# Three root-mean-square norms with tokens on partitions, and weight splits moved ahead of a norm's pieces

## The chip, the cores and the metric

The kernel runs on one NeuronCore of a Trainium2 chip. Its time is device microseconds from launch to end, as the median of several runs. The engines run their own in-order queues and meet through semaphores: TensorE (PE; its weight loads are PEld), VectorE (DVE), ScalarE (ACT), GpSimd (POOL) and SyncE (SP, which issues most DMAs).

## What is computed

A trunk of two layers on an input of 1024 tokens by 1024 features, all float32. Layer 0 mixes tokens by a pooling mixer, layer 1 by an mLSTM (8 heads, here 16 head steps, since the tokens go in two halves). A squared-ReLU MLP follows each mixer. Every sub-layer stands between two norms:

```python
def rmsnorm(x, g):
    return x * lax.rsqrt(jnp.mean(x * x, axis=-1, keepdims=True) + RMS_EPS) * g

for i in range(DEPTH):                       # DEPTH = 2
    hn = rmsnorm(x, mix_pre_g[i])
    y = pool_mixer(hn, ...) if i % 2 == 0 else mlstm_mixer(hn, ...)
    x = x + rmsnorm(y, mix_post_g[i])
    hn = rmsnorm(x, ffn_pre_g[i])
    y = jnp.square(jax.nn.relu(hn @ mlp_w1[i])) @ mlp_w2[i]
    x = x + rmsnorm(y, ffn_post_g[i])
```

## The kernel before

**Layout.** Features lie on partitions: a half of the tokens (`T` = 512) of the activations is eight tiles `y[half][:, k, :]` of 128 features by 512 tokens. A norm therefore sums over partitions as well as over the eight tiles.

**Products.** A float32 product is made of three passes on rounded parts: weights are split into `w_hi` (a cast on ACT, `split_hi`) and `w_lo` (a subtraction on DVE, `split_lo`), activations into `x_hi` and `x_lo`, and PE does hi·hi, hi·lo and lo·hi of 512 columns each (`three_passes`, lines 787 to 789). A weight block must have both parts before PE may start it (`split_ready`). In the head steps, the call that splits `BLOCK["head", j, 2] + 1` makes the parts of the fourth block of head j.

**Norms.** There are 14. Norms 3 to 12 have their squares added on DVE (`acc`, line 1872) and summed over partitions by GpSimd (`partition_all_reduce`, line 1229). Norms 0, 1, 2 and 13 (`FOREGROUND`) are summed by PE: a plain float32 product of a square tile with the tile `ones` gives all 128 partitions the same sums for 512 tokens, in PSUM. Then ACT takes the root of 128x512 into `tot` (`root`, line 1280), DVE its reciprocal of 128x512 into `rstd` (line 1812), and DVE multiplies tile by tile (`normed`, line 1189).

**The opening.** Norm 0 is the norm behind the pooling mixer of half 0, norm 1 the one before the MLP of half 0. PE runs the list `SECOND_POOL`: W are window products of the other half (`window_tile`, line 821), T the sum of norm 0, S the eight sums of norm 1, G the eight groups of the mixer's product. Behind the last G, ACT takes its result out of PSUM (`pool_out`, line 1735), then makes `x_hi` of the first tile (line 1777), DVE its `x_lo` (line 2404), and PE starts the MLP (line 887).

**The head steps.** In step j PE does four weight blocks, each followed by a piece of work of head j-1: `turn`, `updates`, `numerators` (lines 1102 and 1106) and `turn_back` (line 1116). ACT and DVE do their parts in written order. Between them stand `tick(j, part)` calls, which do the pieces of two background norms that the table `LSTM_SLOTS` gives to this place: in steps 2 and 10 `tick(j, 1)` makes the last two additions to `acc`, upon which GpSimd's reduction starts, and in steps 4 and 12 two additions and two residual tiles. `normalize` writes `hnorm`, for which `turn_back` waits. `gate_head(j - 1)` writes `hid_hi` and `hid_lo`, which the output projection (`second_product`, line 851) reads in the step after; the next split is that projection's second block.

**The last head.** `last_head` runs the last head's pieces between pieces of the output projection. ACT does `by_tokens` (waits for `turn`, makes `kw` and `v_tok`) and then `decay_matrix` (four exponentials), for which DVE's `prob` and so PE's numerators wait.

**The end.** Norm 13 closes the kernel. PE sums five tiles into `bank[0]`, then multiplies the eight tiles of `x_last` with the identity into the eight PSUM banks, then the eight scaled tiles on top; so PE adds the residual. ACT copies each bank to `end_sq`, SP stores it.

Of the kernel before, what the change touches and what calls it, by code (L numbers as in the profile page):

```python
# [7 lines left out]
ALU = mybir.AluOpType  # L8
# [5 lines left out]
P = 128  # L14
D = 1024
# [216 lines left out]
def build(nc, x_in, x_tokens, weights, w_first, w_second, vecs_in, consts_in, bands_in, out):  # L232
# [9 lines left out]
    with ExitStack() as ctx:  # L242
# [122 lines left out]

        ones_row = relu_sq
# [44 lines left out]
        end_taken = sem("last_output_taken")  # L411
        x_first_landed = sem("first_old_x_landed")
# [110 lines left out]
        FOREGROUND = (0, 1, 2, 13)  # L523
        BACKGROUND = 3
# [6 lines left out]
        def last_bank(k):  # L531
            return eight[(k + 1) % KT]

# [109 lines left out]
        def _(sp):  # L643
# [105 lines left out]
            for k in range(KT):  # L749
                sp.wait_ge(end_taken, k + 1)  # L750
                sp.dma_start(out[1, k], end_sq[:, k, :]).then_inc(out_stored[1], 16)
# [4 lines left out]
        def _(pe):  # L756
# [14 lines left out]
            def sum_squares(n, tiles=range(KT), o=None, order=tuple(range(KT))):  # L771

                for k in tiles:
                    at = KT * FOREGROUND.index(n) + order.index(k)
                    pe.wait_ge(sq_ready, at + 1)
                    nc.tensor.matmul((o or core[3])[:, :], ones[:, :], (end_sq[:, k, :] if n == NORMS - 1 else squares[k]),
                                     start=(k == order[0]), stop=(k == order[-1])).then_inc(sq_summed, 1)
# [17 lines left out]
            def sum_added():  # L795

                pe.wait_ge(sq_added, KT - 1)
                nc.tensor.matmul(core[3][:, :], ones[:, :], squares[KT - 1], start=True, stop=True).then_inc(sq_summed, 1)
# [96 lines left out]
            def plain_second(layer):  # L895

                for k in range(PLAIN):
# [4 lines left out]
                    for d in ds:  # L902
                        if k == 0 and d < BANKS:
                            pe.wait_ge(plain_taken, layer * HALVES * PLAIN + plain_of_bank(layer, d, 0) + 1)
                        if k == 0 and d == KT - 1 and layer == 0:
# [246 lines left out]
            for step in SECOND_POOL:  # L1152
                if step == "T":
                    sum_added()
                elif step[0] == "W":
                    window_tile(1, int(step[1]))
                elif step[0] == "G":
# [12 lines left out]
            for at, k in enumerate(LAST_D[0:4]):  # L1170
                pe.wait_ge(sq_ready, KT * FOREGROUND.index(NORMS - 1) + at + 1)
                nc.tensor.matmul(bank[0][:, :], ones[:, :], end_sq[:, k, :],
                                 start=(at == 0), stop=False).then_inc(sq_summed, 1)
            pe.wait_ge(end_sums, 3)
            nc.tensor.matmul(bank[0][:, :], ones[:, :], end_sq[:, 3, :], start=False, stop=True).then_inc(sq_summed, 1)
# [1328 lines left out]
```

## Time and profile before

| | us |
|---|---|
| runs (median of 3) | 1971.12 (1970.82 to 1972.35) |
| the profiled execution | 1969.38 |
| its span, first to last instruction | 1967.6 |
| PE busy in it | 1932.8 |
| DVE busy | 1321.8 |
| ACT busy | 1064.2 |
| POOL busy | 91.0 |

The difference of 1.8 between the profiled execution and its span lies outside of the program's instructions. Times below are microseconds from the start of the span. A row of the timeline gives start, length, engine and line, operation, output<-inputs, the shape and the number of instructions merged, and in brackets how long the engine was idle before it and who ended that. `issue` means that the profile shows no releaser. The stages: opening to 66, MLP of layer 0 to about 745, head steps to about 1290, MLP of layer 1 to 1946, end.

### The profile page before, as it was taken

To read this page: it belongs to the slowest core of one execution; us is meant where nothing else is said; L and a number is where in the kernel's file an instruction comes from. 1 tells how busy PE (TensorE), PEld (TensorE's weight loads), DVE (VectorE), ACT (ScalarE), POOL (GpSimd) and SP (SyncE) were. 2 spreads that over 40 slices of the span, in tenths; PEclk is the share of its full clock that TensorE was granted. 3 is DMA by queue.
4 is the path that set the end of the run, shared out by engine and by line. 5 is a ranking of instruction groups with operands and counts; after the bars stand their busy time and mean duration, and the time that the engine had idled before them with its cause. 6 is when DMAs were issued, how large, how long until landed. Compare 5 with 4: busy or idle time off the path is not lost. (4 is left out here: it accounts for less than half of the span.)

```text
span 1967.6 us, 24435 instructions
## 1 busy us (share of the span) xinstructions
PE 1932.8 (98%) x8582; PEld 1546.2 (79%) x8582; DVE 1321.8 (67%) x2070; ACT 1064.2 (54%) x1803; POOL 91.0 (5%) x121
## 2 busy tenths in 40 slices
PE   9999999999999999999999999899999999999999
PEld 6678888888788788878878878777888888878786
DVE  5775656565678877776866857776656565577864
ACT  7645454554445446766756757544554545445433
POOL 0110000000000100110000100021000000000110
PEclk9999999999999999999999999999999999999999
DMA  5344234348633533343223442243524344853353
GB/s 213 103 157 177 103 136 161 134 177 297 229 94 103 197 111 100 118 150 97 97 77 104 135 135 96 66 150 119 191 91 163 132 165 172 315 186 97 112 196 115
DMA packets 80568, 283.94 MB, mean 144 GB/s; under 512 B 9504, under 2 KB 9632, under 8 KB 73536
## 3 DMA queue, kind: packets, MB, share of 16 engines
q1 hardware_dynamic: 64576, 237.86, 34.6%
q0 software_dynamic: 8320, 27.27, 4.3%
q10 hardware_dynamic: 7552, 17.26, 2.7%
q8 instruction: 69, 1.13, 0.2%
q14 instruction: 51, 0.42, 0.1%
HBM read 213.08 MB, written 69.27 MB: 144 GB/s over the span
## 5 line engine op out<-in xcount | busy, mean ns | idle before, releaser
L1807 DVE TENSOR_TENSOR w_lo<-raw,w_hi 128x1024 fp32r<-128x1024 f32 x148 | 185.8, 1256 | 188.5 <-ACT w_hi L1266 185.4
L1266 ACT CAST w_hi<-raw 128x1024 fp32r<-128x1024 f32 x148 | 154.3, 1042 | 195.7 <-PE core L1006 54.1
L787 PE MATMUL bank<-x_hi,w_hi 128*128 128x512 f32 x560 | 227.4, 406 | 7.0 <-issue 6.6
L1452 ACT CAST h_hi<-h_raw 128x512 fp32r<-128x512 f32 x178 | 110.3, 620 | 222.6 <-PE core L1006 137.5
L789 PE MATMUL bank<-x_hi,w_lo 128*128 128x512 f32 x560 | 221.7, 396 | 0.0
L788 PE MATMUL bank<-x_lo,w_hi 128*128 128x512 f32 x560 | 220.6, 394 | 0.0
L2062 DVE TENSOR_TENSOR h_lo<-h_raw,h_hi 128x512 fp32r<-128x512 f32 x178 | 122.9, 690 | 106.9 <-ACT h_hi L1452 106.5
L1004 PE MATMUL core<-h_hi,w_hi 128*128 128x512 f32 x448 | 177.9, 397 | 2.5 <-ACT w_hi L1468 2.5
L1006 PE MATMUL core<-h_hi,w_lo 128*128 128x512 f32 x448 | 176.8, 395 | 0.0
L1005 PE MATMUL core<-h_lo,w_hi 128*128 128x512 f32 x448 | 176.5, 394 | 0.0
L1956 DVE TENSOR_TENSOR w_lo<-sums,w_hi 128x512 fp32r<-128x512 f32 x96 | 66.3, 691 | 99.7 <-ACT w_hi L1294 97.1
L787 PEld LDWEIGHTS bank<-x_hi,w_hi 128*128 128x128 f32 x560 | 105.3, 188 | 32.5 <-issue 10.1
L1004 PE MATMUL bank<-h_hi,w_hi 128*128 128x512 f32 x328 | 129.9, 396 | 0.0
L1006 PE MATMUL bank<-h_hi,w_lo 128*128 128x512 f32 x328 | 129.4, 395 | 0.0
L1005 PE MATMUL bank<-h_lo,w_hi 128*128 128x512 f32 x328 | 129.4, 394 | 0.0
L789 PEld LDWEIGHTS bank<-x_hi,w_lo 128*128 128x128 f32 x560 | 105.1, 188 | 25.7
L788 PEld LDWEIGHTS bank<-x_lo,w_hi 128*128 128x128 f32 x560 | 105.3, 188 | 23.8 <-issue 0.7
L2100 DVE TENSOR_TENSOR w_lo<-w,w_hi 128x512 fp32r<-128x512 f32 x160 | 114.0, 713 | 12.7 <-ACT w_hi L1468 8.7
L887 PE MATMUL bank<-x_hi,w_hi 128*128 128x512 f32 x256 | 104.9, 410 | 3.2 <-DVE x_lo L2404 2.2
L1468 ACT CAST w_hi<-w 128x512 fp32r<-128x512 f32 x160 | 98.4, 615 | 14.8 <-DMA w<-second_pairs 5.7
L1004 PEld LDWEIGHTS core<-h_hi,w_hi 128*128 128x128 f32 x448 | 84.1, 188 | 23.9 <-issue 4.1
L1229 POOL PARTITION_ALL_REDUCE tot<-acc x10 | 34.5, 3447 | 1477.8 <-DVEq L1876 1477.8
(333 smaller groups left out, 4444.2 us busy)
## 6 DMA issues: line engine op xcount, KB each, us to landing
raw<-weights SPq DMA_DIRECT2D x148, 512.0 KB, 3.3
h_pair_dram<-y SPq DMA_DIRECT2D x24, 1792.0 KB, 6.6
h_raw<-h_pair_dram SPq DMA_DIRECT2D x168, 256.0 KB, 2.8
w<-second_pairs SPq DMA_DIRECT2D x32, 768.0 KB, 4.5
x_scratch<-y POOLq DMA_DIRECT2D x48, 256.0 KB, 2.6
raw_odd<-first_pairs SPq DMA_DIRECT2D x12, 1024.0 KB, 7.1
raw<-first_pairs SPq DMA_DIRECT2D x12, 1024.0 KB, 7.1
xold<-x_scratch POOLq DMA_DIRECT2D x40, 256.0 KB, 3.8
```

The source lines that it names most:

```text
L787: nc.tensor.matmul(o, a, hi(t), start=(k == 0), stop=False)
L788: nc.tensor.matmul(o, a, lo(t), start=False, stop=False)
L789: last = nc.tensor.matmul(o, b, hi(t), start=False, stop=(k == n - 1))
L887: nc.tensor.matmul(o, a, XH(half, k), start=(k == 0), stop=False)
L1004: nc.tensor.matmul(o[:, :], a, hh, start=(fresh and first), stop=False, skip_group_check=True)
L1005: nc.tensor.matmul(o[:, :], a, hl, start=False, stop=False, skip_group_check=True)
L1006: ins = nc.tensor.matmul(o[:, :], b, hh, start=False, stop=(final and last), skip_group_check=True)
L1266: nc.scalar.copy(w_hi[:, ROW[u] * T:(ROW[u] + 2) * T], raw[:, (n % RAW) * BLK:(n % RAW + 1) * BLK]).then_inc(hi_ready, 1)
L1452: nc.scalar.copy(h_slot(n)[0], h_raw[:, at % H_RAW, :]).then_inc(h_hi_ready, 1)
L1807: dve.tensor_tensor(w_lo[:, s], raw[:, (n % RAW) * BLK:(n % RAW + 1) * BLK], w_hi[:, s].bitcast(F32), ALU.subtract).then_inc(lo_ready, 1)
L2062: dve.tensor_tensor(lo, h_raw[:, at % H_RAW, :], hi.bitcast(F32), ALU.subtract).then_inc(h_lo_ready, 1)
L2100: dve.tensor_tensor(w_lo[:, s], second_weight(n), w_hi[:, s].bitcast(F32), ALU.subtract).then_inc(lo_ready, 1)
```

## The change

It has three parts.

1. Norms 0, 1 and 13 (`BY_TOKEN`) put tokens on partitions. `token_sums` makes the square tile the stationary operand, in four pieces of 128 tokens, and moves `ones` of 128 columns through; the result is 128 equal columns for each group of 128 tokens. ACT takes the root of one column of each (128x4), DVE the reciprocal of 128x4 and multiplies the identity with it into four diagonal 128x128 tiles in `step_t`; `spread_roots` then multiplies `ones` with the four diagonals, which gives the 128x512 factor in PSUM (`core[3]`, `bank[0]` for norm 13), and `normed` reads it there. `SECOND_POOL` gets R0 and R1 for the two `spread_roots`. The sums of norms 1 and 2 move from `core[3]` to `core[2]`.
2. In the head steps `split_hi` and `split_lo` of the fourth block go ahead of `tick(j, 1)`; for j = 4, 8, 12 `gate_head(j - 1)` goes ahead of `tick(j, 2)`; for the last head `decay_matrix` goes ahead of `by_tokens`.
3. At the end tiles 2, 5 and 7 (`END_ADDED`) get their residual by DVE instead of by PE and ACT. PE does the other five.

```diff
-SECOND_POOL = "W0 T W1 W2 W3 W4 W5 W6 W7 S0 S1 G0 G1 S2 S3 G2 S4 G3 S5 S6 S7 G4 G5 G6 G7".split()
+SECOND_POOL = "W0 T W1 W2 R0 W3 W4 W5 W6 W7 S0 S1 G0 G1 S2 S3 G2 S4 G3 S5 S6 S7 G4 R1 G5 G6 G7".split()
+END_ADDED = (2, 5, 7)
...
+            def token_sums(n, tile, first, last):
+                for c in range(CPH):
+                    ins = nc.tensor.matmul(norm_sums(n)[:, c * P:(c + 1) * P], tile[:, c * P:(c + 1) * P], ones[:, :],
+                                           start=(first and c == 0), stop=(last and c == CPH - 1),
+                                           skip_group_check=True)
+                ins.then_inc(sq_summed, 1)
+
+            def spread_roots(n):
+                for c in range(CPH):
+                    pe.wait_ge(diag_ready, CPH * BY_TOKEN.index(n) + c + 1)
+                    ins = nc.tensor.matmul(norm_roots(n)[:, c * P:(c + 1) * P], ones[:, :], step_t[:, c * P:(c + 1) * P],
+                                           start=True, stop=True)
+                ins.then_inc(rstd_ready, 1)
...
-            for k in range(KT):
-                if k == KT - 1:
-                    pe.wait_ge(std_ready, NORMS)
-                nc.tensor.matmul(last_bank(k)[:, :], ident, x_last[:, k, :], start=True, stop=False)
-            for k in range(KT):
-                pe.wait_ge(end_scaled, k + 1)
-                nc.tensor.matmul(last_bank(k)[:, :], ident, y[1][:, k, :], start=False, stop=True).then_inc(end_done, 1)
+            old(tiles[0])
+            old(tiles[1])
+            spread_roots(NORMS - 1)
+            for at in range(2, len(tiles)):
+                old(tiles[at])
+                add(at - 2)
+            add(len(tiles) - 2)
+            add(len(tiles) - 1)
...
+                    if n in BY_TOKEN:
+                        nc.scalar.activation(token_std.rearrange("p (c o) -> p c o", o=1),
+                                             src[:, :].rearrange("p (c t) -> p c t", c=CPH)[:, :, 0:1], ACT.Sqrt, bias=eps[:, :],
+                                             scale=1.0 / D).then_inc(std_ready, 1)
+                        return
...
-                        by_tokens(j - 1)
                         decay_matrix(j - 1)
+                        by_tokens(j - 1)
...
-                dve.reciprocal(rstd[:, :], tot[:, :]).then_inc(rstd_ready, 1)
+                steps.finish(dve.reciprocal(token_rstd, token_std))
+                for c in range(CPH):
+                    dve.tensor_scalar(step_t[:, c * P:(c + 1) * P], ident, token_rstd[:, c:c + 1], None,
+                                      ALU.mult).then_inc(diag_ready, 1)
...
                     states(j - 1)
+                    split_lo(BLOCK["head", j, 2] + 1)
                     tick(j, 1)
-                    split_lo(BLOCK["head", j, 2] + 1)
...
+                    if j % FT == 0:
+                        gate_head(j - 1)
                     tick(j, 2)
-                    gate_head(j - 1)
+                    if j % FT:
+                        gate_head(j - 1)
...
+                steps.finish(scaled)
+                dve.wait_ge(x_last_landed, 16)
+                dve.tensor_tensor(end_sq[:, k, :], x_last[:, k, :], y[1][:, k, :], ALU.add).then_inc(end_added, 1)
```

DVE in head step 2, from the chunk states (`mid`) to the next head's convolution (`win`). Before:

```order
L2236 SCALAR_TENSOR_TENSOR mid<-mid,inter_b,core1 128x129
L1872 TENSOR_TENSOR acc<-acc,sq 128x512 x2
L1807 TENSOR_TENSOR w_lo<-raw,w_hi 128x1024
L2201 COPY craw<-taps 128x16
L2202 COPY taps<-craw 128x16
L2207 SCALAR_TENSOR_TENSOR win<-craw,vecs,win 128x512 x3
```

Now, with the line numbers of the changed kernel:

```order
L2293 SCALAR_TENSOR_TENSOR mid<-mid,inter_b,core1 128x129
L1858 TENSOR_TENSOR w_lo<-raw,w_hi 128x1024
L1929 TENSOR_TENSOR acc<-acc,sq 128x512 x2
L2258 COPY craw<-taps 128x16
L2259 COPY taps<-craw 128x16
L2264 SCALAR_TENSOR_TENSOR win<-craw,vecs,win 128x512 x3
```

The two additions to `acc`, which release GpSimd's reduction, now stand directly ahead of the convolution instead of ahead of the split. Steps 4, 6, 7 and their twins of the second half change in the same way, with other pieces in the place of the additions.

DVE in head step 4, behind the blocks of head 4. Before:

```order
L2289 TENSOR_TENSOR qs<-qT,inter_b 128x512
L1872 TENSOR_TENSOR acc<-acc,sq 128x512
L1189 SCALAR_TENSOR_TENSOR step_t<-y1,vecs,rstd 128x512
L1884 TENSOR_TENSOR y1<-xold,step_t 128x512
L2274 SCALAR_TENSOR_TENSOR relu_sq<-oT,core0 128x512
L2277 TENSOR_SCALAR hid_hi<-relu_sq,half_norm 128x512
L2278 SCALAR_TENSOR_TENSOR hid_lo<-relu_sq,half_norm,hid_hi 128x512
L1807 TENSOR_TENSOR w_lo<-raw,w_hi 128x1024 x5
```

Now:

```order
L2346 TENSOR_TENSOR qs<-qT,inter_b 128x512
L2331 SCALAR_TENSOR_TENSOR relu_sq<-oT,core0 128x512
L2334 TENSOR_SCALAR hid_hi<-relu_sq,half_norm 128x512
L2335 SCALAR_TENSOR_TENSOR hid_lo<-relu_sq,half_norm,hid_hi 128x512
L1929 TENSOR_TENSOR acc<-acc,sq 128x512
L1236 SCALAR_TENSOR_TENSOR step_t<-y1,vecs,rstd 128x512
L1941 TENSOR_TENSOR y1<-xold,step_t 128x512
L1858 TENSOR_TENSOR w_lo<-raw,w_hi 128x1024 x5
```

The three instructions of `gate_head` went ahead of the norm's three; the splits behind them stay last.

PE at the end, behind the last product of the MLP. Before (ten of the sixteen rows with the identity; the other six are alike but for the bank):

```order
L1172 MATMUL bank0<-end_sq,ones 128x512 x4
L1175 MATMUL bank0<-end_sq,ones 128x512
L1181 MATMUL bank1<-x_last,consts 128x512
L1181 MATMUL bank2<-x_last,consts 128x512
L1181 MATMUL bank3<-x_last,consts 128x512
L1181 MATMUL core0<-x_last,consts 128x512
L1181 MATMUL core1<-x_last,consts 128x512
L1181 MATMUL core2<-x_last,consts 128x512
L1181 MATMUL core3<-x_last,consts 128x512
L1181 MATMUL bank0<-x_last,consts 128x512
L1184 MATMUL bank1<-y1,consts 128x512
L1184 MATMUL bank2<-y1,consts 128x512
```

Now:

```order
L789 MATMUL bank0<-ones,end_sq 128x128 x20
L1217 MATMUL bank1<-x_last,consts 128x512
L1217 MATMUL bank2<-x_last,consts 128x512
L798 MATMUL bank0<-step_t,ones 128x128 x4
L1217 MATMUL core0<-x_last,consts 128x512
L1221 MATMUL bank1<-y1,consts 128x512
L1217 MATMUL core1<-x_last,consts 128x512
L1221 MATMUL bank2<-y1,consts 128x512
L1217 MATMUL core3<-x_last,consts 128x512
L1221 MATMUL core0<-y1,consts 128x512
L1221 MATMUL core1<-y1,consts 128x512
L1221 MATMUL core3<-y1,consts 128x512
```

Sixteen products with the identity became ten, and the four that spread the roots stand behind the second of them.

## Rows read from the trace of the kernel before

**Rows 1.** The page's first part: busy us, share of the span, number of instructions.
```profile
PE 1932.8 (98%) x8582; PEld 1546.2 (79%) x8582; DVE 1321.8 (67%) x2070; ACT 1064.2 (54%) x1803; POOL 91.0 (5%) x121
```
**Rows 2.** Waits of PE over the span: us in total, times, longest.
```profile
PE bank L787 <- issue: 6.6, 7, 1.8
```
**Rows 3.** Timeline of PE in the opening: start, length, what.
```profile
37.69 0.38 PE L821 MATMUL core<-sq,y 128*128 128x128 f32 x2
37.91 0.29 PE L815 MATMUL core<-kw,qT 128*128 128x16 f32 x2
```
**Rows 4.** Timeline of DVE in the opening.
```profile
37.65 3.35 DVE L1812 RECIPROCAL rstd<-tot 128x512 f32<-128x512 f32 x1 [1.28 <-ACT tot L1280]
```
**Rows 5.** Timeline of PE in the opening, two waits.
```profile
48.74 0.48 PE L787 MATMUL bank<-x_hi,w_hi 128*128 128x512 f32 x1 [0.40 <-DVE x_lo L1845]
...
57.69 1.12 PE L776 MATMUL core<-craw,ones 128*128 128x512 f32 x2 [0.21 <-ACT craw L1712]
```
**Rows 6.** Timeline of all engines where the MLP starts.
```profile
65.13 0.60 ACT L1777 CAST x_hi<-y 128x512 fp32r<-128x512 f32 x1
...
66.60 0.47 PE L887 MATMUL bank<-x_hi,w_hi 128*128 128x512 f32 x1 [2.19 <-DVE x_lo L2404]
```
**Rows 7.** Line 1695, a root of 128x4: shortest, median, longest in ns.
```profile
L1695 ACT ACTIVATE small<-small,eps x16: 297/297/298, 779.5 to 1270.0; 128x4 f32<-128x4 f32 x16
```
**Rows 8.** Line 2264, a product of 128x128 with a per-partition factor.
```profile
L2264 DVE TENSOR_SCALAR hnorm<-core,small x64: 339/343/353, 780.3 to 1271.6; 128x128 f32<-128x128 f32 x64
```
**Rows 9.** Timeline of all engines at the end.
```profile
1950.60 2.74 PE L1181 MATMUL bank<-x_last,consts 128*128 128x512 f32 x6
...
1950.80 0.69 ACT L1280 ACTIVATE tot<-bank,eps 128x512 f32<-128x512 f32 x1 [2.94 <-PE bank L1175]
...
1954.91 5.39 DVE L1189 SCALAR_TENSOR_TENSOR y<-y,vecs,rstd 128x512 f32<-128x512 f32 x8
...
1964.53 0.59 ACT L1792 COPY end_sq<-bank 128x512 f32<-128x512 f32 x1 [0.27 <-PE bank L1184]
```
**Rows 10.** DMA issues: line, count, KB each, median us to landing.
```profile
out_tiles<-end_sq SPq DMA_DIRECT2D x8, 256.0 KB, 2.0
```
**Rows 11.** Timeline of ACT in the last head.
```profile
1258.62 1.15 ACT L1675 ACTIVATE kw<-core,cols 128x128 f32<-128x128 f32 x4 [3.35 <-PE core L1080]
...
1261.56 1.28 ACT L1661 ACTIVATE mx_b<-mx_b,cols 128x128 f32<-128x128 f32 x4
```
**Rows 12.** Timeline of DVE in the last head.
```profile
1264.95 0.34 DVE L2236 SCALAR_TENSOR_TENSOR mid<-state,inter_b,core 128x129 f32<-128x129 f32 x1
```
**Rows 13.** A stretch of the last head: length, PE busy, granted clock, DMA share, GB/s.
```profile
1263.60:1267.00 3.40, 3.31 (x13) 0.50 0.27 84
```
**Rows 14.** Timeline of DVE in head step 2.
```profile
799.82 1.49 DVE L1872 TENSOR_TENSOR acc<-acc,sq 128x512 f32<-128x512 f32 x2
802.40 2.38 DVE L1807 TENSOR_TENSOR w_lo<-raw,w_hi 128x1024 fp32r<-128x1024 f32 x1 [1.09 <-ACT w_hi L1266]
```
**Rows 15.** Timeline of PE in head step 2.
```profile
804.88 0.47 PE L787 MATMUL bank<-x_hi,w_hi 128*128 128x512 f32 x1 [0.78 <-issue]
...
810.67 0.66 PE L1116 MATMUL core<-consts,hnorm 128*128 128x128 f32 x4
```
**Rows 16.** Timeline of POOL in head step 2.
```profile
801.46 3.23 POOL L1229 PARTITION_ALL_REDUCE tot<-acc  x1 [111.74 <-DVEq L1876]
```
**Rows 17.** Timeline of DVE at the start of an earlier reduction.
```profile
632.49 2.73 DVE L2100 TENSOR_TENSOR w_lo<-w,w_hi 128x512 fp32r<-128x512 f32 x1 [0.21 <-DVE acc L1872]
```
**Rows 18.** Timeline of ACT in head step 4.
```profile
855.94 0.63 ACT L1545 ACTIVATE qT<-win 128x512 f32<-128x512 f32 x1
```
**Rows 19.** Timeline of DVE in head step 4.
```profile
861.14 1.22 DVE L1807 TENSOR_TENSOR w_lo<-raw,w_hi 128x1024 fp32r<-128x1024 f32 x1
...
874.77 1.22 DVE L1807 TENSOR_TENSOR w_lo<-raw,w_hi 128x1024 fp32r<-128x1024 f32 x1
```
**Rows 20.** Timeline of PE in head step 4.
```profile
874.91 0.50 PE L851 MATMUL bank<-hid_hi,w_hi 128*128 128x512 f32 x1 [1.04 <-DVE hid_lo L2278]
```

More of the change, by code:

```diff
@@ L523, in build @@
         FOREGROUND = (0, 1, 2, 13)
+        BY_TOKEN = (0, 1, 13)
         BACKGROUND = 3
@@ L749, in _ @@
             for k in range(KT):
-                sp.wait_ge(end_taken, k + 1)
+                if k in END_ADDED:
+                    sp.wait_ge(end_added, END_ADDED.index(k) + 1)
+                else:
+                    sp.wait_ge(end_taken, k + 1 - sum(a < k for a in END_ADDED))
                 sp.dma_start(out[1, k], end_sq[:, k, :]).then_inc(out_stored[1], 16)
@@ L769, in keep_clock, with sum_squares @@
                     nc.tensor.matmul(o[:, :], ones[:, :], ones_row[:, :], start=True, stop=True)
-            def sum_squares(n, tiles=range(KT), o=None, order=tuple(range(KT))):
-                for k in tiles:
[L774 to L777, printed above, removed]
+            def token_sums(n, tile, first, last):
[10 more added lines that the diff above has]
+                ins.then_inc(rstd_ready, 1)
+            def sum_squares(n, tiles):
+                for k in tiles:
+                    pe.wait_ge(sq_ready, KT * FOREGROUND.index(n) + k + 1)
+                    if n == 1:
+                        if k == 0:
+                            pe.wait_ge(pooled_ready, KT + 3)
+                        token_sums(n, squares[k], k == 0, k == KT - 1)
+                    else:
+                        nc.tensor.matmul(norm_sums(n)[:, :], ones[:, :], squares[k],
+                                         start=(k == 0), stop=(k == KT - 1)).then_inc(sq_summed, 1)
             def three_passes(g, row, cols_of, hi, lo, tiles, before=None, after=None):
@@ L904, in plain_second @@
                             pe.wait_ge(plain_taken, layer * HALVES * PLAIN + plain_of_bank(layer, d, 0) + 1)
-                        if k == 0 and d == KT - 1 and layer == 0:
+                        if k == 0 and eight[d] is norm_sums(2) and layer == 0:
                             pe.wait_ge(std_ready, 3)
@@ L1156, in _ @@
                     window_tile(1, int(step[1]))
+                elif step[0] == "R":
+                    spread_roots(int(step[1]))
                 elif step[0] == "G":
@@ L1213, in add_residual @@
             for k in range(KT):
-                scaled = steps.begin(normed(eng, step_t[:, :], y[half][:, k, :], post + k))
+                scaled = steps.begin(normed(eng, step_t[:, :], y[half][:, k, :], post + k, norm_roots(0)))
                 low(k)
@@ L1789, in _ @@
             root(norms.pop(0))
-            for k in range(KT):
-                act.wait_ge(end_done, k + 1)
+            for at, k in enumerate(k for k in range(KT) if k not in END_ADDED):
+                act.wait_ge(end_done, at + 1)
                 nc.scalar.copy(end_sq[:, k, :], last_bank(k)[:, :]).then_inc(end_taken, 1)
```

40 lines of the change are left out of this document (29 added, 11 removed).

## The prediction

> **What bounds the kernel now.** I read the page's busy times first: TensorE works 1932.8 of a span of 1967.6, 98%, and VectorE only 67% [rows 1]. So work taken from VectorE or ScalarE is worth nothing in itself; only TensorE's own work, the places where it waits, and the two ends of the kernel count. The waits of TensorE come next. The line that the splits of weights could be blamed for shows 6.6 in seven waits, the longest 1.8 [rows 2]; one of them is the 0.78 in head step 2 [rows 15]. That is the most that splitting earlier can give back. The rest was read place by place, in the timelines of the stretches that the change touches. The profiled execution took 1969.38, 1.74 under the median of 1971.12. I make the sum against the profiled execution and add it to the median.
>
> **Norms 0 and 1 in the opening.** A plain float32 product takes TensorE 0.22 for 128 columns [rows 3], so a square tile costs 4 x 0.22 = 0.88. That is what 512 columns cost in one piece: three products in 2.74 with their modelled end, 0.86 each without it [rows 9]. The sums are therefore free to within 0.02 each. The reciprocal of 3.35 [rows 4] and a root of 128x512, 0.69 [rows 9], become a root of 0.30 [rows 7], a short reciprocal (about 0.2, bounded by 0.3, the ScalarE root of the same shape) and four diagonals of 0.34 or less [rows 8], then four products of 0.22: 0.30 + 0.2 + 1.4 + 0.9 = 2.8 instead of 4.0, so the factor comes about 1 earlier. But TensorE pays 4 x 0.22 = 0.88 for each `spread_roots`, 1.8 for both. What can absorb it are waits: 0.40 and 0.21 [rows 5], with the pipeline's own refill 0.8 to 0.9 for both. The big one, 2.19 ahead of the MLP [rows 6], does not shrink: it runs from TensorE's last group over ScalarE's copy, `x_hi` (65.13 to 65.73) and VectorE's `x_lo`, and R1 stands ahead of that last group, so that the whole chain moves with TensorE. Net 1.8 − 0.85 = **+1.0** (0 if the earlier factor also feeds the groups sooner, 1.8 if the two waits stay).
>
> **Head step 2, and its twin, step 10.** Before, VectorE adds to `acc` from 799.82 to 801.31, GpSimd's reduction starts at 801.46, and `w_lo` starts at 802.40, when ScalarE has written `w_hi`; it takes 2.38 [rows 14, 16]. Its normal length is 1.22 [rows 19]. So it was held by 1.16. If it was held in its first part, then until 803.56, 2.1 behind the start of the reduction of 3.23. An earlier reduction's start shows the same: 2.73 for a subtraction of 512 columns [rows 17], about half of 1.22 if alone, again held by about 2.1. Now `w_lo` comes first. It cannot start before 802.40, since `w_hi` is no earlier, but nothing holds it: it ends at 803.6 and TensorE's wait of 0.78 goes. The two additions follow until about 805.1, and the reduction starts at 805.2. That is exactly where the convolution stands: two copies and three passes over `win` with both tensors in SBUF, 0.3 behind their old place (old start 802.40 + 2.38 = 804.78). If they are held as `w_lo` was, they wait until 805.2 + 2.1 = 807.3, against 805.0: +2.35 with what is late already. Everything down to `hnorm` stands behind them in VectorE's order, and `turn_back` of TensorE (810.67 before [rows 15]) waits for `hnorm`. It then starts at 813.0, though TensorE is there almost 1 earlier. Behind `turn_back` TensorE has no other wait to give this back. So +2.35 each, **+4.7** for both. The low end, if nothing in SBUF is held, is +0.35 each, +0.7.
>
> By the Trainium skill, page "SBUF — State Buffer", section "Who interferes with whom", a VectorE instruction with two SBUF inputs and a GpSimd instruction that reads SBUF exclude each other, and the second to start blocks until the other is done. The row of `w_lo` agrees that there is an exclusion, but by the full reduction it should have run until 804.69 + 1.22 = 805.9, and it ended at 804.78 [rows 14, 16]. Going by that rule, each of the two places would cost 1.1 more.
>
> **Head steps 4 and 12.** ScalarE's `w_hi` comes behind `qT` (855.94 to 856.5 [rows 18]) and takes 1.0, so `w_lo` starts at 857.5 instead of 861.14 [rows 19], and a wait of TensorE of 1.8 (the longest of [rows 2]) is gone. But the pieces of the norm (two additions, two residual tiles, 4.6 in all with their gaps, being what stood between) now stand between `w_lo` and the convolution, which therefore starts at about 863.3 where it started at 861.14 + 1.15 = 862.3: the chain to `hnorm` is +1.0, while TensorE comes 1.8 earlier, and waits there instead, some 3.0. `gate_head` ahead of the next pieces then takes away a wait of 1.04 for `hid_lo` [rows 20], but puts a norm's three passes between it and the next splits: the `w_lo` that stood at 874.77 [rows 19] and ended at 876.0, just in time, ends at about 877.5. I take **+1.3** for step 4 and **+0.8** for step 12, where the old wait was 0.35 longer; −1.8 each if the convolution had slack after all, +2.4 each at worst (1.0 and 1.5 one after the other, nothing absorbed). In the other head steps the swap of split and pieces lies under TensorE's blocks of 5.8 with room on both sides: 0, and 0.3 each if the cover is gone.
>
> **The last head.** ScalarE idles for 3.35 ahead of `kw` and makes the four exponentials only from 1261.56 to 1262.84 [rows 11]. Both they and the load of their table fit into that idle time. So VectorE's `prob`, TensorE's numerators, and the split that follows come earlier; the chunk state at 1264.95 [rows 12] moves to about 1262.4, as `w_hi` and `w_lo` then end there: −2.5. TensorE's 3.31 of work here ran at a granted clock of 0.50, which is 1.2 of 2.4 GHz, behind its wait for the numerators [rows 13]; at the full clock it is up to 1.65 less, of which I take 0.7. **−3.2** (−2.2 to −3.5).
>
> **The end.** TensorE is the bound there: 16 products with the identity from 1950.60, about 0.86 each, and ScalarE's last copy ends at 1964.53 + 0.59 = 1965.12 [rows 9]. Now ten products, 8.6, and 0.9 of spreading: TensorE could be done at 1960.1. The factor is ready at 1950.8 + 0.3 + 0.2 + 1.4 + 0.9 = 1953.6, against 1954.9. VectorE then scales eight tiles in 5.4 [rows 9] and adds three residuals, 0.7 to 0.8 each: 1953.6 + 7.7 = 1961.3. VectorE takes TensorE's place as the bound, the last copy or addition ends at about 1961.6, −3.5. The last stores, 256 KB and 2.0 each [rows 10], go out closer together, which I price at +0.5 (0 to 1), and the sums at +0.1: **−2.8** (−3.4 to −2.3).
>
> **The clock.** The granted clock fell to 0.50 behind one wait of 2.14 in the last head (the numerators') and for 3.4 [rows 13], that is up to 1.7 lost. It did not fall behind the 2.19 of the opening in the profile I have [rows 6]. The change makes four waits of about 3 at `turn_back`. I take one fall, **+1.7** (0 to 6.8).
>
> **Sum**: 1.0 + 4.7 + 1.3 + 0.8 − 3.2 − 2.8 = +1.8; with the clock +3.5. 1971.1 + 3.5 = **1974.6**.
>
> **Rivals.** (a) The convolution is held, but the clock stays: 1971.1 + 1.8 = 1972.9. The opening's wait of 2.19 without a fall speaks for it. Chance 0.13. (b) The convolution is not held: 4.0 less and less of the wait that lowers the clock, so 1968.9. For it speaks that three of five instructions have a factor per partition beside their tensors and the copies are only 16 columns wide; against it, that all the data are in SBUF as those of the held `w_lo`. Chance 0.18. (c) The waits of the heads vanish and nothing is late behind them: 1.0 − 3.2 − 2.8 = −5.0, 1966.1, and as low as 1955.5 if all the waits of [rows 2] and their followers go too. It needs slack between the convolution and `hnorm`, which the rows of step 2 do not show. Chance 0.09. (d) The slower side: all four long waits halve the clock, each for 3.4, 4 x 1.7 = 6.8 on +1.8: 1979.7. It decides from the point where a wait at `turn_back` passes 2.2 or so, the longest that a row shows without a fall; mine are about 3. Chance 0.10. (e) The hold lasts for the whole reduction instead of 2.1: 1.1 more at two places, 1974.6 + 2.2 = 1976.8. `w_lo` speaks against it, since it ended early. Chance 0.05. It is what the page named above would give, and the trace does not agree.
>
> The forecast itself has 0.45: held at both places, one or two falls of the clock, 1973 to 1977.
>
> **How the numbers follow.** A measurement of this kernel can tell about 0.2%, 3.9, from no change: faster is below 1967.2, slower above 1975.1. Faster: (c), and a quarter of (b): 0.14. Slower: (d), (e), and somewhat under half of the forecast, whose centre lies half a microsecond below the line: 0.35. The same: 0.51. The range reaches from (b) and the upper part of (c), 1966.5, to 1978.0, which leaves out (d) and the lower half of (c).
>
> **What would show it.** In the changed kernel's trace: `w_lo` of step 2 takes 1.2 and TensorE's wait behind it is gone; the reduction starts right behind it at about 805 and one of the convolution's instructions lasts 2 too long; TensorE waits about 3 for `hnorm` in steps 2, 4, 10 and 12; the granted clock is 0.50 behind one of them; in the last head the numerators stand directly behind the updates and the chunk state is 2.5 earlier, relative to the head's start; the last copy ends about 3.5 earlier relative to the last sum, and VectorE, not TensorE, ends last. The MLP's first wait is still 2.2, 1.0 later. The forecast is wrong if the convolution runs at its normal length beside the reduction (then 1969), or if the waits at `turn_back` stay under 1.

## The result, and the profile after

The changed kernel takes 1977.58 us (median of 8 runs, 1975.88 to 1980.02) against 1970.97 for the kernel before (8 runs, 1969.66 to 1972.35): 1.0037 times as long, 95% interval 1.0027 to 1.0047. It is slower by 5.3 to 9.3 us, 6.6 in the medians. The forecast was 1974.6, that is +3.5, and the likeliest single verdict was "the same". The profiled execution took 1979.08, 1.5 above the median, with a span of 1977.3. All differences below are between the profiled executions unless a median is named.

Three words are used throughout. The *lag* at a place is how much later the same product of TensorE starts in one trace than in the other. A *fall* is a stretch in which the granted clock is 0.50, that is 1.2 GHz in place of 2.4. An instruction is *held* when it lasts longer than the same instruction does elsewhere in the trace.

The page's first part, as in [rows 1]: TensorE's busy time is 6.7 longer, while the change takes work away from it at the end.

```profile
PE 1939.5 (98%) x8678; PEld 1560.3 (79%) x8678; DVE 1317.2 (67%) x2085; ACT 1060.7 (54%) x1800; POOL 91.2 (5%) x121
```

TensorE's waits (us in total, times, longest). The waits for a split, 6.6 in [rows 2], are down to 1.8, as was meant; a new line stands first in their place.

```profile
PE core L1151 <- DVE hnorm L2321: 13.8, 5, 3.5
PE bank L945 <- ACT h_plain L1407: 2.8, 2, 2.4
...
PE bank L822 <- issue: 1.8, 2, 1.1
```

**Head step 2.** The timeline of VectorE and GpSimd. Compare it with [rows 14, 16]: `w_lo` takes 1.22 instead of 2.38, the additions stand behind it, the reduction starts at 808.02, and the second copy of the convolution, 16 columns wide, takes 2.10 where its twin, which was under way when the reduction started, took 0.17.

```profile
805.24 1.22 DVE L1858 TENSOR_TENSOR w_lo<-raw,w_hi 128x1024 fp32r<-128x1024 f32 x1 [2.68 <-ACT w_hi L1313]
806.39 1.48 DVE L1929 TENSOR_TENSOR acc<-acc,sq 128x512 f32<-128x512 f32 x2
808.01 0.17 DVE L2258 COPY craw<-taps 128x16 f32<-128x16 f32 x1
...
808.02 3.27 POOL L1276 PARTITION_ALL_REDUCE tot<-acc  x1 [116.43 <-DVEq L1933]
...
808.22 2.10 DVE L2259 COPY taps<-craw 128x16 f32<-128x16 f32 x1
```

TensorE's rows at `turn_back` in steps 2, 4, 10 and 12. In [rows 15] the same row had no wait.

```profile
815.90 1.11 PE L1151 MATMUL core<-consts,hnorm 128*128 128x128 f32 x4 [3.48 <-DVE hnorm L2321]
875.54 0.66 PE L1151 MATMUL core<-consts,hnorm 128*128 128x128 f32 x4 [3.05 <-DVE hnorm L2321]
1100.23 1.11 PE L1151 MATMUL core<-consts,hnorm 128*128 128x128 f32 x4 [3.22 <-DVE hnorm L2321]
1160.95 1.12 PE L1151 MATMUL core<-consts,hnorm 128*128 128x128 f32 x4 [3.05 <-DVE hnorm L2321]
```

The four products take 1.11 or 1.12 in three of the four places, 0.66 in the other. That is the clock: at 875.54 it had not fallen yet. Stretches behind these waits, and behind two that the kernel before has as well (columns: from and to, length, busy us of PE, PEld, DVE, ACT and POOL with their instructions, then the granted clock, DMA share and GB/s):

```profile
815.50:819.00 3.50, 3.04 (x9) 2.28 (x10) 3.35 (x7) 3.47 (x5) 0.00 (x0) 0.53 0.28 62
876.40:880.60 4.20, 3.88 (x10) 3.08 (x11) 4.01 (x8) 0.98 (x3) 0.00 (x0) 0.59 0.39 125
1100.20:1106.20 6.00, 5.90 (x16) 4.52 (x17) 5.28 (x7) 4.70 (x6) 0.00 (x0) 0.53 0.27 90
1161.00:1167.50 6.50, 6.44 (x17) 4.94 (x18) 6.03 (x9) 3.26 (x6) 0.00 (x0) 0.52 0.25 81
68.00:72.00 4.00, 4.00 (x9) 2.50 (x10) 3.92 (x6) 3.54 (x8) 0.00 (x0) 0.57 0.02 4
1353.60:1358.60 5.00, 4.62 (x13) 3.65 (x14) 2.46 (x4) 2.63 (x4) 1.87 (x1) 0.66 0.38 129
```

All four long waits are followed by the 1.2 GHz level, and so are the MLP's first wait in the opening (2.19, at full clock in the kernel before, [rows 6]) and the wait of 2.37 for `h_plain` near 1354.

**The ledger.** I compared the starts of the same product in both traces (the 7632 products of 512 columns with `w_hi` or `w_lo` stand in the same order) and took the lag at a few places. The third column is what the lag grows by while the products behind a wait run at the half clock, the second is all the rest.

| stretch | lag grows by, clock apart | by the half clock | forecast |
|---|---|---|---|
| opening, to the MLP's first product | +1.4 | +1.5 | +1.0 |
| layer 0, a wait that absorbs | −0.5 | | |
| head step 2 | +2.8 (−0.73, then +3.54) | +0.9 | +2.35 |
| head step 4 | −0.1 (−2.00, +3.11, −1.19) | +1.5 | +1.3 |
| head step 10 | +2.5 (−0.83, +3.28) | +2.0 | +2.35 |
| head step 12 | −0.3 (−2.03, +3.12, −1.40) | +2.2 | +0.8 |
| last head (with the fall that went, [rows 13]) | −3.4 | | −3.2 |
| MLP of layer 1 | +0.3 | +1.6 | |
| end | −2.6 | | −2.8 |
| sum | +0.1 | +9.7 | +1.8, and +1.7 for the clock |

The sum is, but for rounding, the 9.7 between the spans. Without the falls behind its own waits the change is worth nothing; with them it costs 9.7 in this execution and 6.6 in the medians (this execution is 1.5 above its median, the one profiled before 1.6 below its own).

The +0.1 still holds one gain by the clock. In the last head the kernel before ran its numerators at 0.50 [rows 13]; from the first of them to the next block they took 3.60 (1263.67 to 1267.27), and here 2.53 at full clock, a new wait of 0.56 among them. So about 1.6 of the −3.4 is a fall that went. An estimate from these numbers: with no fall in either kernel the change would cost about 1.7.

**The last head.** The same stretch as [rows 11, 12], from VectorE and ScalarE: the exponentials now stand ahead of `kw`, and the first chunk state, which came 6.3 behind `kw`'s start, comes 3.7 behind it.

```profile
1270.47 1.28 ACT L1712 ACTIVATE mx_b<-mx_b,cols 128x128 f32<-128x128 f32 x4
1272.46 0.69 DVE L2276 SCALAR_TENSOR_TENSOR prob<-core,mx_b 128x512 f32<-128x512 f32 x1 [0.83 <-PE core L1115]
1272.51 1.15 ACT L1726 ACTIVATE kw<-core,cols 128x128 f32<-128x128 f32 x4 [0.77 <-issue]
1276.25 0.35 DVE L2293 SCALAR_TENSOR_TENSOR mid<-state,inter_b,core 128x129 f32<-128x129 f32 x1
```

**The end**, as in [rows 9]. TensorE's first product with the identity stands at 1963.09 here, at 1950.60 before. From there to the end of ScalarE's last copy it was 14.5, and it is 10.8. ScalarE's copy of TensorE's last tile ends last (1973.86); VectorE is through 0.4 earlier, but it sets the pace, since TensorE waits for each scaled tile.

```profile
1963.29 0.26 ACT L1323 ACTIVATE ssq<-bank,eps 128x4 f32<-128x4 f32 x1 [3.11 <-PE bank L789]
1963.59 0.18 DVE L1866 RECIPROCAL rs<-ssq 128x4 f32<-128x4 f32 x1 [1.95 <-ACT ssq L1323]
1963.80 0.87 DVE L1868 TENSOR_SCALAR step_t<-consts,rs 128x128 f32<-128x128 f32 x4
1964.81 1.05 PE L798 MATMUL bank<-step_t,ones 128*128 128x128 f32 x8
1965.90 2.06 DVE L1236 SCALAR_TENSOR_TENSOR y<-y,vecs,bank 128x512 f32<-128x512 f32 x3 [1.23 <-PE bank L798]
...
1973.27 0.59 ACT L1843 COPY end_sq<-core 128x512 f32<-128x512 f32 x1 [0.52 <-PE core L1221]
```

### The profile page after: what moved, and what is told of

It reads as the page before. It is cut to its first block and busy times, and to the rows that moved or that the text cites. A ratio compares the mean times of both kernels' runs of the same rounds, so it can differ in the third digit from the quotient of the medians.

```text
span 1977.3 us, 24651 instructions
## 1 busy us (share of the span) xinstructions
PE 1939.5 (98%) x8678; PEld 1560.3 (79%) x8678; DVE 1317.2 (67%) x2085; ACT 1060.7 (54%) x1800; POOL 91.2 (5%) x121
## 5 line engine op out<-in xcount | busy, mean ns | idle before, releaser
L1520 ACT CAST w_hi<-w 128x512 fp32r<-128x512 f32 x160 | 98.6, 616 | 13.8 <-DVE w L2137 4.6
```

## The experiments

Three theories stood: (A) the head steps' new order costs all of the loss, by a held convolution and a late chain, and each long wait brings a fall of the clock with it; (B) the norms with tokens on partitions cost it; (C) the falls are chance and only the waits count. The kernel before ran at 1969.90, 1970.65 and 1970.59 in the three groups of four.

### Which part costs it

**e1_old_order** is the changed kernel with the old order in the head steps, on VectorE (shown) and on ScalarE.

```diff
-                    split_lo(BLOCK["head", j, 2] + 1)
                     tick(j, 1)
+                    split_lo(BLOCK["head", j, 2] + 1)
...
-                    if j % FT == 0:
-                        gate_head(j - 1)
                     tick(j, 2)
-                    if j % FT:
-                        gate_head(j - 1)
+                    gate_head(j - 1)
```

> The changed kernel with the head steps back in their old order (split behind the pieces, gate_head behind them in every step); the last head, the three norms and the end stay changed. My ledger of the changed kernel's trace puts +11.6 us on head steps 2, 4, 10 and 12 (extra waits of TensorE for hnorm of 3.0 to 3.5 and the half clock behind each). If that is right, all of it goes: 1971.0 + 2.5 (opening) - 3.4 (last head) - 2.6 (end) = about 1967.5, between 1966 and 1969.5, and no wait over 2.0 in the head steps. Rival (the norms with tokens on partitions cost it, the order is innocent): 1975 or more.

Measured: 1966.31 (10 runs), 0.9981 of the kernel before (0.9971 to 0.9990). That is 3.6 faster than before, where the whole change is 6.6 slower. So (A) holds as to the place, and (B) is out: the order in the head steps costs about 10. Its waits of TensorE have the split first again, and none for `hnorm` above 1:

```profile
PE bank L822 <- issue: 7.1, 7, 1.9
```

One part of the expectation missed: there is a fall in its head steps, behind the wait for a split in step 12 (1.91); the kernel before has 1.78 there, without a fall.

**e3_opening_old_too** also takes norms 0 and 1 back.

```diff
-        BY_TOKEN = (0, 1, 13)
+        BY_TOKEN = (13,)
...
```

> As the first kernel, and norms 0 and 1 of the opening also as before; only the last head's swap and norm 13 with the end stay changed. Theory: 1971.0 - 3.4 - 2.6 = 1965. The difference to the first kernel is the opening's price: theory 1.0 to 1.4 at full clock (two times four products of 0.22 less what waits absorb), up to 2.5 with a fall of the clock behind the MLP's first wait. Rival: the opening costs nothing in itself and the 2.5 in the profile was the clock alone; then both kernels agree within 0.5.

Measured: 1963.71 (8 runs), 0.9970 (0.9959 to 0.9981), 6.2 faster than the kernel before. The two parts that are left, the last head and the end, are worth what the ledger says: the last head −3.37 in its trace too. Against e1 the opening costs 2.6 in the medians. The traces, at full clock in both at this place, put it at 1.2; with intervals of about 2 either way on each median I go by the traces. So the opening is not free, and the second case of the expectation is out, as far as one pair of traces can tell.

### The held convolution

**e2_adds_behind** makes the two additions of steps 2 and 10 behind `normalize`, so that the reduction doesn't meet the convolution.

```diff
-                    tick(j, 1)
+                    if j not in (2, 10):
+                        tick(j, 1)
                     conv(j, 1)
                     denominators(j - 1)
                     normalize(j - 1)
+                    if j in (2, 10):
+                        tick(j, 1)
```

> The changed kernel, but in steps 2 and 10 VectorE makes the two additions that release GpSimd's reduction behind normalize, not ahead of the convolution. If the convolution is held by the reduction (theory), the copy of taps takes 0.2 instead of 2.1, the two waits of about 3.4 at turn_back go, with the half clock behind them: 1977.6 - 2 x (2.4 + 0.35 + about 1.5) = about 1969, with up to 1.5 more if the earlier split is then worth its 0.75. Rival 1 (the waits cost only themselves, the clock fell by chance): 1972.5. Rival 2 (the additions themselves made the chain late, not the hold): the same gain as the theory in time, but then a held instruction would stand elsewhere in these steps at equal cost.

Measured: 1973.18 (10 runs), 1.0017 (1.0008 to 1.0026). That is 3.3 slower than the kernel before beside it, where the changed kernel was 6.6 slower: a gain of 3.3 (4.4 between the plain medians of the two), not the 8.6 expected. The copy of `taps` takes 0.17 again and the wait at `turn_back` is gone, so the hold was the cause of that wait. But a new wait stands behind `turn_back`. VectorE, GpSimd and TensorE in step 2:

```profile
813.55 1.23 DVE L1858 TENSOR_TENSOR w_lo<-raw,w_hi 128x1024 fp32r<-128x1024 f32 x1
813.55 4.31 POOL L1276 PARTITION_ALL_REDUCE tot<-acc  x1 [120.98 <-DVEq L1933]
814.69 2.73 DVE L2342 TENSOR_TENSOR mx_b<-consts,mx_b 128x512 f32<-128x512 f32 x1
...
814.87 0.48 PE L822 MATMUL bank<-x_hi,w_hi 128*128 128x512 f32 x1 [2.16 <-ACT w_hi L1313]
```

The `w_lo` of the block behind `turn_back`, which used to follow `hnorm` at once, came 1.6 late, and this wait (2.16, in step 10 2.03) halved the clock as well, in both steps. The reduction was held too: it started together with `w_lo` and took 4.31 instead of 3.27. I had moved the additions from in front of one thing that TensorE waits for to in front of the next one.

**e5_adds_behind_split** puts them one place further, behind that split.

```diff
                     split_lo(BLOCK["head", j, 3] + 1)
+                    if j in (2, 10):
+                        tick(j, 1)
```

> The changed kernel, but in steps 2 and 10 VectorE makes the two additions behind the split that follows normalize (in the last experiment of this kind they stood ahead of it, and TensorE got a new wait of 2.2 to 2.3 for that split). Theory (the hold of the convolution is all that was wrong there): no wait over 1 in steps 2 and 10, the chain 0.75 earlier than in the kernel before, since the split stands ahead: 1977.6 - 5.2 - 5.2 (the waits and one fall of the clock each) - up to 0.8 more = about 1967 to 1970, against the kernel before at 1969.9 on this chip. Rival (the reduction, now beside mx_b and qs, holds something that TensorE needs): a new wait of 2 in the step after, and 1972 or more.

Measured: 1968.87 (10 runs), 0.9991 (0.9981 to 1.0000). That is 1.8 faster than the kernel before beside it, so 8.4 better than the changed kernel (8.7 between the plain medians): the theory's case. The reduction now holds `qs`, which costs TensorE only 0.7 at the next head's first split:

```profile
811.50 1.22 DVE L1858 TENSOR_TENSOR w_lo<-raw,w_hi 128x1024 fp32r<-128x1024 f32 x1
812.63 1.49 DVE L1929 TENSOR_TENSOR acc<-acc,sq 128x512 f32<-128x512 f32 x2
814.26 0.69 DVE L2342 TENSOR_TENSOR mx_b<-consts,mx_b 128x512 f32<-128x512 f32 x1
814.87 2.73 DVE L2346 TENSOR_TENSOR qs<-qT,inter_b 128x512 f32<-128x512 f32 x1
```

The hold is 1.9 or 2.0 beyond the instruction's own length in these places (copy 2.10 for 0.17, `mx_b` in e2 and `qs` in e5 2.73 for 0.69). Steps 2 and 10 together are worth 8.4: the 2.8 and 2.5 of the ledger, the rest the clock (2.9 there).

### Steps 4 and 12

**e6_steps_4_12_new** and **e7_gate_first** start from the kernel of e3. The first has the whole new order in steps 4 and 12 only, the second only `gate_head` ahead of the next pieces:

```diff
+                    if j % FT == 0:
+                        gate_head(j - 1)
                     tick(j, 2)
-                    gate_head(j - 1)
+                    if j % FT:
+                        gate_head(j - 1)
```

> The kernel of e3_opening_old_too (1963.7) with the new order (split ahead of the pieces, gate_head ahead of the next ones) in steps 4 and 12 alone. Theory: two waits of 3.0 at turn_back in place of 1.9 ahead of it, hid_lo's wait of 1.0 to 1.4 gone: about +0.1 each at full clock, and a fall of the clock of 1.7 each: 1963.7 + 3.6 = 1967.3. Rival (the falls are not tied to these waits): 1964.

> The kernel of e3_opening_old_too with only gate_head ahead of the pieces in steps 4, 8 and 12. Forecast of the prediction: hid_lo's wait goes (1.0 and 1.4) but the split behind comes 1.5 late: about -0 to +0.5 per step. What the changed kernel's trace suggests: the wait goes and nothing comes in its place, -1.1 each in steps 4 and 12: 1961.5.

Measured: e6 1967.49 (10 runs), 0.9985 (0.9976 to 0.9995), as forecast, with both falls in the trace. e7 1964.32 (6 runs), 0.9970 (0.9959 to 0.9982), not the 1961.5. The split in step 4 of e7, and TensorE, which waits for it:

```profile
875.03 0.69 DVE L1939 TENSOR_TENSOR y<-xold,step_t 128x512 f32<-128x512 f32 x1
876.52 1.23 DVE L1856 TENSOR_TENSOR w_lo<-raw,w_hi 128x1024 fp32r<-128x1024 f32 x1 [0.79 <-ACT w_hi L1308]
...
877.85 0.47 PE L817 MATMUL bank<-hid_hi,w_hi 128*128 128x512 f32 x1 [1.40 <-issue]
```

The wait of [rows 20] is gone (−1.2), and 1.5 is lost behind it for the next split; in step 12 it is −1.6 and +1.6. This is just what the prediction said of it ("ends at about 877.5", here 876.52 + 1.23 = 877.75). In the changed kernel it can't be seen, because TensorE, at half clock, comes late enough. Its trace had misled me: a fall of the clock had covered a wait. That it was the fall and nothing else is argued from the two traces; no profile has the new order in step 4 at full clock.

**e8_combined** is e7 with e5's order in steps 2 and 10, **e9_best** the same without `gate_head`'s move.

> The kernel of e7 with the split ahead and the additions behind the next split in steps 2 and 10. If e5's theory and e7's second case both hold: -0.75 twice and -1.1 twice on 1963.7: 1960.0. If only one of them: 1961.5 to 1962.2.

> The kernel of e8_combined with gate_head behind the pieces again. e7 against e3 showed hid_lo's wait of 1.2 gone and a new one of 1.36 for the split behind it, 1.5 in all at two places, so the swap costs 0.3 each: 1964.0 - 0.6 = 1963.4 by that. Rival (the swap is worth something once steps 2 and 10 are clean): 1964.5 or more. The two can hardly be told apart by medians; the ledger of steps 4 and 12 in the trace tells them apart.

Measured: e8 1964.03 (6 runs), 0.9967 (0.9956 to 0.9979); e9 1963.98 (5 runs), 0.9966 (0.9952 to 0.9980). Neither differs from e3's 0.9970. In e9's trace steps 2 and 10 gain 1.0 and 1.1 up to `turn_back` and lose 0.6 and 0.7 at the next head's first block, whose split now waits for the additions and the held `qs`. So the earlier split is worth 0.4 a step at best in any order tried here, too little for these medians to show.

### The end

**e10_end_by_pe** is e3 with TensorE adding seven of the eight tiles.

```diff
-END_ADDED = (2, 5, 7)
+END_ADDED = (7,)
```

> The kernel of e3_opening_old_too, but only tile 7 gets its residual by VectorE; TensorE does seven (tile 7's bank holds the factor, so it can't be TensorE's). Theory (TensorE bounds the end, and each tile it gives up saves two products of 0.86 less what VectorE adds): 14 products and 0.9 instead of 10 and 0.9: the end 3.4 longer by TensorE, of which the changed end loses back its stores' crowding (about 0.9): 1963.7 + 2.5 = 1966.2. Rival (the gain came from the factor being early, not from sharing): 1963.7 to 1964.2.

Measured: 1967.68 (10 runs), 0.9985 (0.9975 to 0.9994), a ratio 0.0015 above e3's, or 2.9 us. The rival, that the early factor makes the gain, is out: from the first product with the identity (1948.65) to the end of the last copy it is 14.0, against 10.8 in e3.

```profile
1948.65 1.88 PE L1212 MATMUL bank<-x_last,consts 128*128 128x512 f32 x4
...
1962.02 0.58 ACT L1838 COPY end_sq<-core 128x512 f32<-128x512 f32 x1 [0.27 <-PE core L1216]
```

So the sharing of the additions makes most of the end's gain; against the 14.5 of the kernel before, what is left for the small root, the spreading and the one shared tile together is 0.5.

### What a wait does to the clock

Three kernels measured the disputed price by itself. They are the kernel before with products of `hnorm` repeated (the same values again), which makes TensorE wait at `turn_back` in nine head steps that had no wait there: graded numbers in e4, six each in e11, twelve each in e12.

```diff
+                for _ in range(EXTRA.get(j + 1, 0)):
+                    steps.finish(dve.tensor_scalar(hnorm[:, 0:LC], core[2][:, 0:HEAD_DIM], small[:, 7, 0:1], None,
+                                                   ALU.mult))
```

> The kernel before, with repeated products of hnorm's first 128 columns (0.3 to 0.4 each, the same values again) in nine head steps that wait for nothing now: 3 of them ahead of step 3's hnorm, 5 in step 5, 7 in 6, 9 in 7, 11 in 9, 4 in 11, 6 in 13, 8 in 14, 10 in 15. TensorE then waits at turn_back, from below 1 to about 4. Theory: behind each wait above about 2.2 the granted clock falls to 0.50 and costs 1.2 to 2.2 more; below 1.5 it never falls. So the total is the sum of the waits plus about 1.7 for each of the four or five long ones: some 7 over the waits. Rival: the falls have nothing to do with a wait's length; then some short waits show one and some long ones none, and the time is the sum of the waits within 2.

> The kernel before with six repeated products ahead of hnorm in each of nine head steps (3, 5, 6, 7, 9, 11, 13, 14, 15). By the graded run a wait of TensorE is 0.385 for each less 1.2: about 1.1 each. Theory: hardly any fall of the clock behind these (0 to 2 of 9): 1970.3 + 8 or 9 x 1.1 = 1980 (1979 to 1983). Rival (any wait can bring a fall): 1985 or more.

> The same with twelve in each of the nine steps: waits of about 3.4. Theory: every one is followed by a fall that costs 1.7: 1970.3 + 9 x (3.4 + 1.7) = 2016, and nine stretches at 0.50. Rival (falls are a matter of chance at any length): about half of them, 2008; or none beyond those that were there: 2001.

Measured: e4 1999.89, e11 1996.35, e12 2024.92 (4 runs each), that is +30.0, +25.8 and +54.3 on the kernel before. The waits for `hnorm` in e11 and e12 (in total, times, longest):

```profile
PE core L1118 <- DVE hnorm L2269: 10.8, 9, 1.5
```
```profile
PE core L1118 <- DVE hnorm L2269: 31.6, 9, 3.8
```

e11 missed its forecast of 1980 by 16. Some 5 of that I had overlooked in the trace of e4: behind a wait at `turn_back` TensorE waits again, 0.52, for the next block's split, which stands behind `hnorm` on VectorE. Some 7 are falls: four that the kernel before does not show, one of them behind waits of only 1.1 and 0.8 in a row. The other 3 or 4 lie between the profiled execution (1992.8) and the median; more falls would make them, which no profile shows. In e4, too, the expectation was too sharp: a wait of 1.5 had a fall ("below 1.5" was my limit) and one of 2.7 had none. In e12 every one of the nine waits is followed by a fall, five of them by a second directly behind the first; its time is 9 above the 2016 expected, by these second falls and by the 0.52 behind each wait, which that sum also left out. Stretches behind the first two waits of e12 (3.75 and 3.4) and behind the same waits of e11 (1.43 and 1.13):

```profile
841.50:848.00 6.50, 5.85 (x16) 4.47 (x17) 6.06 (x11) 0.63 (x1) 1.07 (x2) 0.53 0.35 121
928.70:933.70 5.00, 4.12 (x14) 3.19 (x15) 4.82 (x9) 1.84 (x3) 0.00 (x0) 0.66 0.32 105
```
```profile
839.50:846.00 6.50, 5.49 (x25) 4.37 (x26) 6.06 (x11) 1.99 (x3) 1.07 (x2) 1.00 0.37 121
923.10:929.10 6.00, 5.03 (x23) 3.99 (x24) 5.82 (x10) 4.23 (x5) 0.00 (x0) 1.00 0.27 90
```

I then read the granted clock in the 7 us behind every wait of TensorE of 1.3 or more in all 14 profiles, from 20 us on, and counted behind how many it was 0.50. A wait is here the figure in brackets of TensorE's row:

| wait of TensorE | waits | with a fall behind it |
|---|---|---|
| 1.3 to 1.99 | 29 | 4 |
| 2.0 to 2.4 | 37 | 21 |
| 2.6 to 2.9 | 3 | 2 |
| 3.0 and more | 18 | 18 |

A fall costs up to 1.7, and a second one directly behind it up to 1.7 more; it is less where a fall begins within the wait, as at 1099 in the changed kernel. Of the four below 2.0 three had another wait of 0.5 right behind them (so had some without a fall); the fourth is the 1.91 of e1. Between 2.0 and 2.4 the same wait goes both ways: the MLP's first wait, 2.19 in every profile, was followed by a fall in 6 of 14, the wait of 2.37 for `h_plain` in 8 of 14. What decides there stays open. These stretches are from behind the first of them, in e7 and in e8:

```profile
66.20:71.20 5.00, 4.50 (x11) 2.80 (x11) 4.86 (x8) 4.52 (x9) 0.00 (x0) 0.66 0.00 0
```
```profile
66.20:71.20 5.00, 4.49 (x16) 2.90 (x16) 4.86 (x8) 4.53 (x9) 0.00 (x0) 1.00 0.00 0
```

So (C) is right for waits of 2.0 to 2.4 and wrong for the change's own, which are 3.0 and more.

## Where the prediction failed, and what in it held

**The step that failed is the clock's.** It said: "The change makes four waits of about 3 at `turn_back`. I take one fall, +1.7 (0 to 6.8)." The waits came as forecast (3.48, 3.05, 3.22, 3.05), and each was followed by a fall, two of them by a double one: 6.6 in the ledger for these four, where the sum had 1.7. The rival (d), all four, was the right case in its mechanism; its 1979.7 is 2.1 above the median, because steps 4 and 12 cost less than the sum has. It got 0.10 because I compared waits of 3 with one of 2.19 that happened to have no fall in the one profile I had. Two waits of 2.1 to 2.3, one with a fall and one without, say that the matter is open at that length; for 3 they say that it can't be less likely. The likeliest case should have been (d). The other 3.1 of half clock in the profile are the falls behind the MLP's first wait and the wait for `h_plain`. Each comes in about half of the profiles, so I take them as chance, and in the median only in part.

**The held convolution**: right in place, instruction and size. The reduction started right behind the additions (808.02), and a copy of the convolution was held until 810.32. From `w_lo` to the last passes of the convolution VectorE fell 2.4 further behind in both steps (`w_lo` 802.40 and 805.24, `win` 804.99 and 810.23), forecast 2.35. TensorE's own lag grew by 2.8 in step 2, since it entered this step 0.4 less late than VectorE. Rival (b), not held, is out. Rival (e), by which the hold lasts the whole reduction, is out too: the reduction ended at 808.02 + 3.27 = 811.29 and the copy at 810.32. The Trainium skill, page "SBUF — State Buffer", section "Who interferes with whom", is borne out in that the two engines exclude each other, and not in that the second is held for the whole instruction. In these traces VectorE's instruction came free about 2.1 behind the start of a reduction of 3.2. The hold goes the other way too: a reduction that started beside a `w_lo` of 1.23 took 4.31, and what VectorE did next came free 1.1 later, by as much as the reduction was late (e2, `mx_b`).

**Steps 4 and 12**: forecast +1.3 and +0.8, measured −0.1 and −0.3 beside the clock. The chain (+1.0) came out at +1.1 (−2.00 and +3.11), and the late split (+1.5) is there in e7; but the half clock behind the wait made TensorE late by itself, and the late split cost nothing on top. Falls and late operands were added in the sum, and they overlap. That this error of 2.4 lay the other way than the clock's brought the forecast nearer to the measured time; that is luck.

**The opening**: forecast +1.0, measured +1.4 (1.2 in e1). The two small waits absorbed 0.6 to 0.8, and the MLP's wait stayed 2.19, as said. **The last head**: −3.4 for −3.2, of which the clock made about 1.6 (0.7 was taken) and the order the rest (2.5 was taken): right in sum, by two errors that cancel. **The end**: −2.6 for −2.8 (the prediction's own terms, −3.5, +0.5 and +0.1, give −2.9). It is 3.75 shorter to the last copy, and the last stores give 1.0 of it back (0 to 1 was the price), plus 0.2 for the sums.

**The whole**: these parts without the clock come to +0.1 where +1.8 was forecast, so the sum of the mechanism was right within 2, and the clock, forecast at 1.7, was 9.7 in the profiled execution and, by difference, about 6.5 in the medians. The mean granted clock that is on record for single runs agrees: 0.993 to 0.995 in the 8 runs of the changed kernel, 0.997 to 0.999 in 59 of 60 runs of the kernel before.

## What to carry to other kernels

Work that an idle engine can do early is free only if what it goes ahead of has slack: the earlier split took away 4.8 of waits for a split (6.6 to 1.8) and made waits for `hnorm` of 13.8 out of 1.0, because a norm's pieces now stood in front of what the next chain needed. Price a stall of TensorE by its length and by what it does to the clock behind it: here 3 us of waiting cost 3 and up to 1.7 more. And before moving an instruction that starts a GpSimd reduction, look at which VectorE instruction comes next; put it in front of one that nobody waits for, or one that is not held. Look also for places where falls already happen: a trace at half clock can hide a wait that comes back when the clock does (e7). The two parts that paid (an exponential moved into idle time, the last additions shared by two engines) stand at places where, as I read it, no other work absorbs the gain; alone they make the kernel 6.2 us faster (e3, 0.9970, 0.9959 to 0.9981).

## What the runs showed of the hardware

- A VectorE instruction that meets GpSimd's reduction (3.23 to 3.27 alone) comes free about 2.1 behind the reduction's start, not at its end, and a copy with a single 16-column input is held like a two-input subtraction (0.17 became 2.10). Where VectorE's instruction was there first, the reduction is held: 4.31 beside a `w_lo` of 1.23 (e2), 3.78 beside `mx_b` of 0.69 (e5).
- Not every VectorE instruction is held. In the kernel before, three `mid` updates (two inputs, one of them `core` in PSUM) ran at their normal length right behind a reduction's start at 906.93, and the `w_lo` after them, both inputs in SBUF, took 1.82 for 1.22:

```profile
906.93 3.23 POOL L1229 PARTITION_ALL_REDUCE tot<-acc  x1 [33.57 <-DVEq L1876]
907.67 0.73 DVE L2236 SCALAR_TENSOR_TENSOR mid<-mid,inter_b,core 128x129 f32<-128x129 f32 x2
908.44 1.82 DVE L1807 TENSOR_TENSOR w_lo<-raw,w_hi 128x1024 fp32r<-128x1024 f32 x1
```

- The granted clock fell behind all 18 waits of TensorE of 3.0 or more, behind 21 of 37 between 2.0 and 2.4, and behind 4 of 29 from 1.3 to 1.99. A fall costs up to 1.7 whatever the wait's length.
- The clock goes with the spread of one kernel's runs, 2.7 before and 4.1 after. Over the 60 runs of the kernel before in the three groups, those with a mean granted clock of 0.999 took 1969.24 on average (18 runs), with 0.998 1970.37 (25), with 0.997 1971.44 (16), and the one with 0.996 1973.36. That it is the waits of 2.19 and 2.37, which fall in one execution and not in the next, is an inference from the 14 profiles; runs without a profile don't show where the clock fell.
